# One hybrid decoder layer on one core: the down bias added per expert in the bank of the down products, and w_out for the full tiles wholly in split products

## The reference

```python
def moe_ffn(x, router_w, router_b, w_gu, b_gu, w_down, b_down):
    logits = x2.astype(jnp.float32) @ router_w.astype(jnp.float32) + router_b.astype(jnp.float32)
    top_vals, top_idx = lax.top_k(logits, TOP_K)
    gates = jax.nn.softmax(top_vals, axis=-1).astype(x.dtype)
    ...
    def expert_block(args):
        xb, e = args
        gu = xb @ w_gu[e] + b_gu[e]
        gate = jnp.minimum(gu[:, :D_FF], SWIGLU_LIMIT)
        up = jnp.clip(gu[:, D_FF:], -SWIGLU_LIMIT, SWIGLU_LIMIT)
        h = (up + 1.0) * (gate * jax.nn.sigmoid(SWIGLU_ALPHA * gate))
        return h @ w_down[e] + b_down[e]
    ...
def hybrid_layer(...):
    proj = x @ w_in + b_in
    ...
    mixed = (jax.nn.sigmoid(m_a) * y_a + jax.nn.sigmoid(m_b) * y_b) @ w_out
    x = layernorm(DEEPNORM_ALPHA * x + mixed, ln1_g, ln1_b)
    x = layernorm(DEEPNORM_ALPHA * x + moe_ffn(x, router_w, router_b, w_gu, b_gu, w_down, b_down), ln2_g, ln2_b)
```

## Time and profile before

| | before |
|---|---|
| median of 3 runs | 1194.64 us (1194.02 to 1195.1) |
| the profiled execution | 1193.83 us, span 1192.1 us |
| PE busy | 1144.1 us (96%) |
| DVE busy | 520.6 us (44%) |
| ACT busy | 260.0 us (22%) |
| moved by DMA | 443.78 MB, mean 372 GB/s |

### The profile page before, as it was taken

How to read it: one execution, slowest core, us unless ns; L and a number is a source line. 1 busy time by engine, 2 the same in 40 slices (tenths; PEclk the granted TensorE clock), 3 DMA queues, 4 the chain that set the end, 5 groups by cost and what they waited for, 6 DMA issues and landing times.

```text
span 1192.1 us, 13955 instructions
## 1 busy us (share of the span) xinstructions
PE 1144.1 (96%) x5682; PEld 555.9 (47%) x5682; DVE 520.6 (44%) x989; ACT 260.0 (22%) x405; POOL 3.3 (0%) x13
## 2 busy tenths in 40 slices
PE   9999999999999999999999989999999999999994
PEld 8999999663333333333333323333333333333331
DVE  6788788883333333333333332333333333333336
ACT  4655655411111111111111111111111111111112
POOL 1000000000000000000000000000000000000000
PEclk9999999999999999999999999999999999999998
DMA  9866964768999999999999999999999999999994
GB/s 231 263 207 174 265 194 130 290 280 347 384 428 426 427 428 428 428 426 428 428 427 428 427 428 427 428 426 428 429 427 427 426 429 428 426 429 427 427 425 161
DMA packets 93853, 443.78 MB, mean 372 GB/s; under 512 B 7912, under 2 KB 65400, under 8 KB 68062
## 3 DMA queue, kind: packets, MB, share of 16 engines
q1 hardware_dynamic: 93614, 442.41, 92.1%
q10 hardware_dynamic: 176, 0.48, 0.1%
HBM read 441.34 MB, written 1.53 MB: 372 GB/s over the span
## 4 chain that ended last, share of the span: by engine, by line
PE 65%; DMA 24%; DVE 7%; ACT 2%; issue 2%; SPq 0%; DVEq 0%; POOL 0%; ACTq 0%; POOLq 0%
PE PS L949 25%; DMA ring<-in_w_gu 19%; PE PS L990 13%; PE PS L737 8%; PE PS L854 6%; DMA ring<-in_w_down 4%; PE PS L876 3%; PE PS L758 2%; DVE w_lo L1096 2%; PE PS L862 1%; DVE tiles L1139 1%; PE PS L869 1%; PE PS L913 1%; PE PS L768 1%; PE PS L1030 1%
## 5 line engine op out<-in xcount | busy, mean ns | idle before, releaser
L949 PE MATMUL PS<-ring,mid 128*64 128x512 f32 x1920 | 422.0, 593 | 20.4 <-DMA ring<-in_w_gu 19.8
L949 PEld LDWEIGHTS PS<-ring,mid 128*64 128x64 f32 x1920 | 135.8, 137 | 299.8 <-issue 258.5
L990 PE MATMUL PS<-ring,mid 128*64 128x512 f32 x952 | 211.3, 595 | 0.0
L1421 DVE TENSOR_SCALAR PS<-PS 128x512 f32<-128x512 f32 x30 | 21.0, 700 | 353.1 <-PE PS L949 353.1
L737 PE MATMUL PS<-x_hi,w_hi 128*128 128x320 f32 x448 | 140.5, 314 | 1.9 <-ACT tiles L555 1.1
L737 PE MATMUL PS<-x_lo,w_hi 128*128 128x320 f32 x448 | 138.4, 309 | 0.0
L737 PE MATMUL PS<-x_hi,w_lo 128*128 128x320 f32 x448 | 138.4, 309 | 0.0
L1403 DVE TENSOR_TENSOR ys<-PS,ys 64x512 fp32r<-64x512 f32 x64 | 44.1, 689 | 193.9 <-ACT ys L642 185.6
L990 PEld LDWEIGHTS PS<-ring,mid 128*64 128x64 f32 x952 | 65.6, 137 | 129.5 <-issue 129.5
L1139 DVE SCALAR_TENSOR_TENSOR x_tok<-PS,gate,x_tok 128x1024 f32<-128x1024 f32 (+1 forms) x93 | 115.2, 1276 | 20.9 <-PE PS L876 20.9
L633 ACT ACTIVATE mid<-PS 128x512 f32<-128x512 f32 x30 | 17.9, 597 | 418.8 <-DVE PS L1421 418.8
(11 more groups left out here) (243 smaller groups left out, 756.2 us busy)
## 6 DMA issues: line engine op xcount, KB each, us to landing
ring<-in_w_gu SPq DMA_DIRECT2D x124, 2048.0 KB, 41.7
ring<-in_w_down SPq DMA_DIRECT2D x59, 2048.0 KB, 40.3
raw<-in_w_in SPq DMA_DIRECT2D x56, 512.0 KB, 5.8
ring<-in_w_down SPq DMA_DIRECT2D x9, 1024.0 KB, 11.9
ring<-in_w_gu SPq DMA_DIRECT2D x8, 1024.0 KB, 7.5
ring<-in_w_out SPq DMA_DIRECT2D x4, 1024.0 KB, 5.0
x_tok<-in_x_prompt SPq DMA_DIRECT2D x2, 512.0 KB, 4.9
x_tok<-in_w_down SPq DMA_DIRECT2D x1, 1024.0 KB, 12.3
```

The costliest lines, as they stand in the source:

```text
L949: last = mm(PS[64 * a:64 * a + 64, b, :], xgT[:, 2 * (u % 2) + j, u // 2, :], w[2 * j + b][:, a * HALF:(a + 1) * HALF], start=False, stop= ...
L990: last = mm(PS[64 * a:64 * a + 64, XB, :], hT[:, j, u, :], w[j][:, a * HALF:(a + 1) * HALF], start=(u == 0 and j == 0), stop=(u == 1 and j ...
L1421: dve.tensor_scalar(gm, gm, LIMIT, None, ALU.min).then_inc(gm_ok, 1)
```

## The change

Seven edits in one. (1) All of K of tiles 0 and 1 is split in w_out; tile 2 stays fp32. (2) The split operands of the first half are made early: ACT copies a row block of w_out in each of the blocks 4 to 7 (`EARLY`), and the first half of mixT in block 7; DVE subtracts right behind. Those of the second half are made after block 7. (3) PE's order in w_out: tile 2 to block 6, first half of tile 0, last block of tile 2, first half of tile 1, second halves of tiles 0 and 1. (4) The operands lie in other slots, so units 2 and 10 are no longer loaded during the projection but after `first_free`; unit 3 and the halves of units 4 and 11 come earlier, unit 9 later. (5) `gated_bias`, the transposes of the gates, their copies and splits go. (6) `add_down_bias`: one product per expert, `esel4` by the third part of `bias4`, starts the bank of the down products, and these then only accumulate. (7) `begin` only scales x1, and the counts of `c_done` fall by three.

```diff
-HALVED = (0, 1, 2, 4, 10)
+HALVED = (0, 1, 4)
...
+EARLY = {4: 2, 5: 3, 6: 0, 7: 1}
...
-                    if k < 6:
-                        load_half(k // 2, k % 2).then_inc(unit_in[k // 2], 16)
-                    elif k < KC:
-                        load_out(k - 6)
-                    else:
-                        load_half(10, k - KC).then_inc(unit_in[10], 16)
+                        load_out(0)
...
             load_unit(6)
-            load_unit(9)
+            load_unit(3)
+            sp.wait_ge(first_read, 1)
+            sp.wait_ge(outlo_ok, 2 * HALF_K)
+            load_half(4, 1).then_inc(unit_in[4], 16)
+            load_half(FREED, 0).then_inc(freed_in, 16)
             sp.wait_ge(block_ok, KC + 1)
             load_unit(5)
             sp.wait_ge(first_free, 1)
-            load_unit(3)
-            load_half(4, 1).then_inc(unit_in[4], 16)
-            load_half(FREED, 0).then_inc(freed_in, 16)
+            load_unit(2)
+            load_unit(10)
             sp.wait_ge(wout_done, 5)
             load_unit(8)
+            load_unit(9)
...
+                if j == 3 and c in EARLY:
+                    k = EARLY[c]
+                    act.wait_ge(wout_in[k // 2], 16)
+                    act.activation(out_hi[:, k, :], out_rows(k // 2)[:, k % 2, :], ACT.Copy).then_inc(outhi_ok, 1)
+                if j == 4 and c == KC - 1:
+                    act.wait_ge(wcur_ok, KC)
+                    act.wait_ge(block_ok, HALF_K + 1)
+                    for t in range(2):
+                        act.activation(mix_s[:, t, 0], mix_of(t), ACT.Copy).then_inc(mixhi_ok, 1)
...
-            project(0, 0, range(HALF_K, KC - 1))
-            pe.wait_ge(block_ok, KC + 1)
-            for a in range(2):
-                last = project(2, a, [KC - 1])
-            last.then_inc(wout_done, 1)
-            project(0, 0, [KC - 1])
-            project(0, 1, range(HALF_K, KC))
-            pe.wait_ge(mixlo_ok, 1)
-            for a in range(2):
-                project_split(0, a).then_inc(wout_done, 1)
+            last.then_inc(second_read, 1)
+            pe.wait_ge(outlo_ok, 2 * HALF_K)
             pe.wait_ge(mixlo_ok, 2)
             for a in range(2):
-                last = project_split(1, a)
+                project_split(0, a, False)
+            pe.wait_ge(block_ok, KC + 1)
+            project(KC - 1).then_inc(wout_done, 1)
+            for a in range(2):
+                last = project_split(1, a, False)
             last.then_inc(first_free, 1)
-            for a in range(2):
-                project(1, a, range(HALF_K, KC)).then_inc(wout_done, 1)
+            pe.wait_ge(mix2lo_ok, 2)
+            for t in range(2):
+                for a in range(2):
+                    project_split(t, a, True).then_inc(wout_done, 1)
...
-            def gated_bias(t, bank):
-
-                t0, n = TILES[t]
-                for a in range(2):
-                    rows = slice(64 * a, 64 * a + 64)
-                    mm(PS[0:n, bank + a, :], gT_hi[rows, t0:t0 + n], bias4[rows, 2, :], start=True, stop=False)
-                    last = mm(PS[0:n, bank + a, :], gT_lo[rows, t0:t0 + n], bias4[rows, 2, :], start=False, stop=True)
-                last.then_inc(c_done, 1)
+            def add_down_bias(par, bank):
+
+                mm(PS[:, bank, :], chosen(par), bias4[:, 2, :], start=True, stop=False)
...
+            dve.wait_ge(second_read, 1)
+            out2_low(0)
+            out2_low(1)
             for t in range(2):
-                dve.wait_ge(mixhi_ok, t + 1)
...
+                dve.wait_ge(mix2hi_ok, t + 1)
+                dve.tensor_tensor(mix2_lo[:, HALF_K:KC, t * P:(t + 1) * P], mix_of(t, slice(HALF_K, KC)),
+                                  mix2_hi[:, t].bitcast(F32), ALU.subtract).then_inc(mix2lo_ok, 1)
+            out2_low(2)
+            dve.wait_ge(wout_done, 1)
+            out2_low(3)
```

More of the change, by code:

```diff
@@ L294, in hybrid_layer @@
         HALF_K = KC // 2
[L295 to L300, removed]
+        out_hi = place("out_hi", [P, HALF_K, D], 10 * slot, F32R)
+        out_lo = place("out_lo", [P, HALF_K, D], slot, F32R)
+        out2_hi = place("out2_hi", [P, HALF_K, D], 9 * slot, F32R)
+        out2_lo = place("out2_lo", [P, HALF_K, D], 8 * slot, F32R)
         def half_of(n, h):
@@ L314, in hybrid_layer, with mix_of @@
         mix_s = place("mix_s", [P, 2, 2, HALF_K, P], X1, F32R)
-        def mix_of(t):
-            return mixT[:, 0:HALF_K, t * P:(t + 1) * P]
+        mix2_hi = place("mix2_hi", [P, 2, HALF_K, P], 7 * slot + 8 * D, F32R)
+        mix2_lo = place("mix2_lo", [P, KC, T], MID, F32R)
+        def mix_of(t, ks=slice(0, HALF_K)):
+            return mixT[:, ks, t * P:(t + 1) * P]
         ln2g, ln2b = half_of(UNITS * NE, 0)[:, 0:D], half_of(UNITS * NE, 0)[:, D:2 * D]
@@ L751, in _, with project, project_split @@
             pe.wait_ge(proj_taken, KC + 7 * KC)
-            def project(t, a, ks):
-                t0, n = TILES[t]
[L755 to L759, removed]
+            def project(k):
+                t0, n = TILES[2]
+                for a in range(2):
+                    last = mm(PS[64 * a:64 * a + n, 4, :], mixT[:, k, t0:t0 + n],
+                              out_rows(k // 2)[:, k % 2, a * HALF:(a + 1) * HALF], start=(k == 0), stop=(k == KC - 1))
                 return last
-            def project_split(t, a):
+            def project_split(t, a, second):
                 cols = slice(a * HALF, (a + 1) * HALF)
                 for k in range(HALF_K):
[L766 to L769, removed]
+                    if second:
+                        pe.wait_ge(out2lo_ok, k + 1)
+                        x_hi2, x_lo2 = mix2_hi[:, t, k, :], mix2_lo[:, HALF_K + k, t * P:(t + 1) * P]
+                        w_hi2, w_lo2 = out2_hi[:, k, cols], out2_lo[:, k, cols]
+                    else:
+                        x_hi2, x_lo2 = mix_s[:, t, 0, k, :], mix_s[:, t, 1, k, :]
+                        w_hi2, w_lo2 = out_hi[:, k, cols], out_lo[:, k, cols]
+                    for n, (x, w) in enumerate(((x_hi2, w_hi2), (x_lo2, w_hi2), (x_hi2, w_lo2))):
+                        last = mm(PS[:, 2 * t + a, :], x, w, start=(not second and k == 0 and n == 0),
+                                  stop=(second and k == HALF_K - 1 and n == 2))
                 return last
@@ L1201, in _ @@
                     bias_low(c, 0)
+                if c in EARLY:
+                    out_low(c, 0)
+                if c == KC - 1:
+                    out_low(c, 1)
+                    for t in range(2):
+                        dve.wait_ge(mixhi_ok, t + 1)
+                        dve.tensor_tensor(mix_s[:, t, 1], mix_of(t), mix_s[:, t, 0].bitcast(F32), ALU.subtract)\
+                           .then_inc(mixlo_ok, 1)
                 taken(7)
@@ L1214, in _ @@
                         last.then_inc(bias_ok, 1)
+                if c in EARLY and c < KC - 1:
+                    out_low(c, 1)
                 ahead(10)
@@ L1390, in part, with begin @@
                 return dve.value_load(items[0:1, 1, ds(i, 1)], min_val=0, max_val=NB)
-            def begin(t, count, bank):
+            def begin(t):
                 n = TILES[t][1]
-                dve.wait_ge(c_done, count)
-                return stt(halves(y_acc[0:n, t, :]), halves(x1[0:n, t, :]), ALPHA, PS[0:n, bank:bank + 2, :],
-                           ALU.mult, ALU.add)
+                return dve.tensor_scalar(y_acc[0:n, t, :], x1[0:n, t, :], ALPHA, None, ALU.mult)
             def low_part(count, bank=XB, halfway=False):
@@ L1410, in one_expert @@
                 s = i % 2
[L1411 to L1415 removed]
+                if i > 0 and i != LOOP + 2:
                     low_part(2 * it + i)
@@ L1428, in one_expert @@
                 if i == 0:
+                    dve.wait_ge(gate_ok, 1)
                     dve.wait_ge(items_ok, 1)
+                    dve.wait_ge(used, 5)
                 for q, t in enumerate((2, 1, 0)):
                     count = 6 * it + (3 * i + q + 1)
-                    last = begin(t, count, CB[t]) if i == 0 else add(t, before, count, CB[t])
+                    last = begin(t) if i == 0 else add(t, before, count, CB[t])
                     last.then_inc(c_taken, 1)
```

82 lines of the change are left out of this document (31 added, 51 removed).

## The result

| | before | after |
|---|---|---|
| median of 6 runs | 1194.33 us (1193.2 to 1195.1) | 1200.89 us (1199.44 to 1204.51) |
| the profiled execution | 1193.83 us, span 1192.1 us | 1200.88 us, span 1199.1 us |
| mean granted clock of PE | 0.994 | 0.985 |

The ratio is 1.0058, 95% interval 1.0048 to 1.0068: **slower by 0.58%**, where 1193.3 us in a range of 1190.5 to 1197.0 were forecast. The prediction was wrong in size and in sign.

The account below looks back on a forecast made before the run. The prediction took the DMA loads to bound the kernel after the last dry stretch near 300 us. Expert 0's end gave -1.5 us and the tail +0.2, so -1.3 us: 1193.3 us for the median, range 1190.5 to 1197.

Parts of the forecast that it names:

- the cost of PE's longer wait in the router: In the router: 3.65 us more of PE waiting, counted at full clock; rival with lower clock 1199 us, chance 0.13.
- w_out on PE: PE's split products save 3.1 us; w_out ends at 251.4 us instead of 254.4, yet expert 0 starts about 0.65 us later.
- The router follows PE: Rival, faster: DVE's new wait ahead of tile 0 vanishes, start up to 3.0 us earlier, 1190 to 1192 likelier; chance 0.18.
- The early halves and the loads: ACT copies and DVE subtractions in blocks 4 to 7, and 9.8 us of moved loads fitting dry DMA stretches: cost nothing.
- Expert 0: First expert on PE: gate transposes and gated bias products go, one bias product comes; -2.2 us.
- The other bias products: 31 more products of 0.23 us, one an expert, hidden beside the slower loads; uncovered they would cost 7.1 us.
- The tail: Near the last loads, the second of two bias products comes after PE's wait for w_down: +0.23 us.
- The sum without the clock: Whole kernel at full clock: -1.5 us from expert 0, +0.2 from the tail, -1.3 us; median 1193.3 us, chance 0.64.

Follow-up runs that it names:

- e1_warm: Changed kernel with ten products of constants into an unread bank, filling PE's wait between the logits of tile 2 and tile 0; 1192.8 us, ratio 0.9988.
- e6_gap: Kernel before, with only tile 1's normalisation held up by four more passes of its statistics on DVE; 1204.27 us, ratio 1.0083.
- e8_gap_warm: Kernel before with the same hold-up as e6_gap, and the wait filled by 12 products of constants; 1197.2 us, ratio 1.0026.
- e4_order: Changed kernel with PE finishing tile 0 ahead of tile 1 in w_out; 1190.22 us, ratio 0.9971.
- e2_bias_only: Kernel before with edits (5) to (7) alone, w_out as it was; 1192.34 us, ratio 0.9983.
- e7_triple: e4_order with each of the 32 down bias products issued three times, the last one counting; 1192.17 us, ratio to the kernel before 0.9983.
- e3_wout_only: Changed kernel with the gated bias of before, so edits (1) to (4) alone; 1201.13 us, ratio 1.0061.
- e5_tail: e4_order with the last expert's bias product moved ahead of the second down unit of the expert before it; 1189.66 us, ratio 0.9961.

## Why the prediction was wrong

- **The step that failed: the cost of PE's longer wait in the router.** The prediction saw the wait ("3.65 us more of waiting between short transposes and logits"), named what it could do to the clock, worked out 1199 us with a range of 1194 to 1205, gave it 0.13, and put the wait into its own sum at the full clock. The waits came as seen (0.67 and 2.56 us in the router's rows above); the clock did not stay full behind them, and the router takes 20.2 us from there on for 13.2. e1_warm, e6_gap and e8_gap_warm show this rival: measured 1200.89, and 8.1 us of it return when the wait is filled.
- **Why it was rejected.** The prediction took the empty end for the only place where the clock falls in the trace of before. It is not. In the middle of the experts PE waits for 2.86 us, right behind 32 down products of 512 columns, and the clock falls there too, to 0.57 over 710 to 712 us and 0.58 over 712 to 714; the gather behind the wait takes 4.59 us instead of 2.94 (a row of PE, then a stage, both of before):

```profile
710.10 4.59 PE L854 MATMUL PS<-x,onehot 128*64 128x512 f32 x12 [2.86 <-DVE esel L1320]
...
712.00:714.00 2.00, 2.00 (x6) 0.23 (x4) 0.00 (x0) 0.00 (x0) 0.00 (x0) 0.58 1.04 442
```

The 1.00 that the earlier trace rows show from 304 to 1160 us is a mean over the stage and hides this. The DMA moves 426 and 442 GB/s meanwhile, so no load is held up there; in the router the fall holds up expert 0 and the loads that wait for it. So the trace of before did hold the evidence that a mid-kernel wait of this length can bring the clock down. The full clock through the router of before, where PE was busy for 16.0 of 16.5 us, showed only that transposes and logits *without waits* hold it. And the end, where the clock is still 1.00 from 1177 to 1180 without a matmul, was read as if it held for the router. The Trainium skill (TensorE: Matmul & The Clock Gate, "Why this matters for your kernels") says that idle gaps between bursts of matmuls in mid kernel send the clock back to the lower level. The trace after agrees: 0.50 from 258 us on, behind a wait of 2.56 us. What the prediction cites of transposes no run here tests by itself.

- **w_out on PE** was right: 251.96 us for 251.4, with the start 0.34 later. Tile 0 on DVE at 246.62 (246.1 forecast), tile 1's aggregate at 257.05 (256.65).
- **The router follows PE** did not hold: DVE has a wait of 3.38 us on PE ahead of tile 0 and works in a row from there, as the forecast said. e4_order shows what removes it, which no step of the prediction asked for.
- **The early halves and the loads** fitted, as costed: DVE still has a wait of 2.04 us on ACT behind its subtractions in block 7 (4.43 before), and the DMA moves 433 GB/s over 240 to 248, 427 from 309 on.
- **Expert 0** was right: from its first product to that of expert 1 it takes 306.38 - 278.81 = 27.6 us, against 300.88 - 270.92 = 30.0 before: -2.4 for -2.2. e2_bias_only shows the same by itself.
- **The other bias products** are hidden, as costed (e7_triple).
- **The tail** was mis-sized: +0.23 forecast for a product in the open, 0.43 us from its start to the next product (1171.52 to 1171.95), and 0.6 in all.
- **The sum without the clock**: e1_warm is the changed kernel with this one term taken out, and it gave 1192.8 us where 1193.3 was forecast. Its first product of expert 1 stands at 299.05 us, near the 299.3 of the prediction. So the rest of the sum held in its steps too, not by luck. What stays open is 0.2 us between the take-up of the DMA and its last load, and why behind the same wait of 2.56 us the clock is low for 10 us in one kernel's profile and for 17 in another's.

## What to carry to other kernels

When a stage gets faster on PE, look for what PE does next: if it then stands waiting ahead of work that the next stage needs, price that work at the 1.2 GHz level too (7 to 8 us here, for a wait of 2.56 us). Don't take a full clock in a gapless trace as evidence for one with a gap, and don't take it from the mean of a long stage: go through the granted clock in stretches of 2 us and look for waits like the one that you expect. First order the work so that the wait doesn't arise (finish the tile that the next engine wants first: 1200.89 to 1190.22 us), and only else fill it with products that nobody reads (1192.8). A saving on an engine counts only from the moment at which the next engine can start: 3 us less on PE gave nothing until tile 0 came out ahead of tile 1.

## What the runs showed of the hardware

- In the router the granted clock fell in each of the three kernels profiled with a wait of 2.56 to 2.75 us there and nothing to fill it: during the wait in the changed kernel and in e6_gap, 0.8 us behind it in e3_wout_only. It stayed at the lower level for 10 us (e3_wout_only) to 17 us (the other two), with PE busy in nearly all of it.
- It returned in the same mix of short work in which it had been low, in e3_wout_only while PE was at mask counts of 32 columns and a few bias products, in the changed kernel during the gather.
- Products of 512 columns right ahead of a wait don't prevent the fall. The wait of 2.86 us in the middle of the experts stands in all ten traces. Behind it the clock was low for some 3 us in six of them, for some 10 us in e5_tail and e7_triple, and not at all in e3_wout_only and e8_gap_warm. So neither the fall nor its length follows from the wait alone.
- Much shorter waits did it near the start. PE turns x there in 24 transposes and then waits for 0.43 us. In the four traces in which a load holds up the transposes as well, for 0.31 to 0.88 us (the changed kernel, e1_warm, e2_bias_only, e7_triple), the clock is at 0.50 for some 3 us from about 12 us on; in the six others it stays at 1.00. The first w_out product stands at 221.93 to 222.53 us in the three of the four that have the changed projection, and at 221.46 to 221.57 in e3_wout_only, e4_order and e5_tail, which have the same projection without this fall.
- Late in the kernel before, PE waits for loads again and again, for up to 1.25 us, between streams of 16 products of 512 columns, and the clock stays at 1.00. One such wait, in PE's timeline:

```profile
954.42 3.65 PE L949 MATMUL PS<-ring,mid 128*64 128x512 f32 x16 [1.24 <-DMA ring<-in_w_gu]
```

- With ten products of 512 columns in the router's wait (2.56 us of work, e1_warm), the clock stayed at 1.00 through all of the router that followed.
